# Second mixer of a two-model kernel: halves of queries and keys exchanged by transfers instead of a product, and two pairs of score banks for the differential attention

## The chip, the core and the metric

The kernel runs on one core of a Trainium2 chip. A core has TensorE for matrix products (in the profile PE, its weight loads PEld), VectorE (DVE), ScalarE (ACT), GpSimd (POOL) and SyncE (SP, which issues most transfers). They run side by side and meet at semaphores. TensorE writes to PSUM, which has eight banks of 128 partitions by 512 fp32 numbers. The metric is device time in microseconds; less is better.

## The reference, cut to what matters

The program computes a first transformer block and then a second model of two layers, for one sequence of 512 tokens of width 1024. The first layer of the second model is the "even mixer": a state-space scan (Mamba 2) and a differential attention side by side. The change touches the attention's queries and keys, and how its scores are scheduled.

```python
def rope(x, pos):
    d = x.shape[-1]                      # 64
    half = d // 2
    ang = pos.astype(F32)[:, :, None] * inv_freq
    x1, x2 = xf[..., :half], xf[..., half:]
    return jnp.concatenate([x1 * cos - x2 * sin, x2 * cos + x1 * sin], axis=-1)

def diff_attention_group(q, k, v, pos, layer, lambdas, subln):
    q = rope(q.reshape(bsz, s, 2 * hh, d), pos).reshape(bsz, s, hh, 2, d)   # hh = 8 heads, d = 64
    k = rope(k.reshape(bsz, s, 2 * hh, d), pos).reshape(bsz, s, hh, 2, d)
    ...
        p1 = masked_softmax(einsum('bqhd,bkhd->bhqk', q1b, k1) * scale, mask)
        p2 = masked_softmax(einsum('bqhd,bkhd->bhqk', q2b, k2) * scale, mask)
        return einsum('bhqk,bkhe->bqhe', p1 - lam * p2, vf)
    o = rms_norm_2(o, subln) * (1.0 - lam_init)
```

Each head has two queries and two keys of 64 numbers. The rope multiplies a vector by a cosine and adds its two halves of 32, exchanged and one of them negated, times a sine.

## The kernel before

Activations lie with features on partitions and the 512 tokens along the free axis. Every dense product is done in split precision: a weight panel is loaded by SP to `w_raw`, ScalarE casts it to `w_hi` (line 1296), GpSimd subtracts to `w_lo` (line 588), and TensorE does three products for each tile of 128 features (lines 617 to 619, or 638 to 640 where tokens are on the partitions of the result). Five slots of weights rotate. The order of panels is written out in `ORDER`, and each engine's program is written by hand in the order in which it runs; an engine that waits at a semaphore holds everything behind it in its program.

In the second mixer two loops of 32 steps each run one after the other, and dense products are filled in between ("units", one generator step each, about 0.70 us of TensorE).

The scan (lines 948 to 960 on TensorE): in step s TensorE does half of the step's units, then `segments(s+1)` (lines 935 and 937, banks 4 and 5), then the rest of the units, waits for `s_m`, and does the value products (line 958). ScalarE takes the exponential of the segments (line 1580), VectorE multiplies them (line 2295). `SSM_FILL` says how many units a step takes. `segments(s+1)` waits until ScalarE has read the banks, by `s_e`. The units compute the queries and keys of head groups 0 and 1 (`dqk0`, `dqk1`, four tiles each) and their values (`dv0`, `dv1`). On ScalarE and VectorE, `DONE_SSM` says after which step a tile is dealt with: ScalarE copies it from PSUM to `QD` (line 1566) and casts the next panels; VectorE does the rope (lines 2264, 2266, 2267).

The attention (`attend_diff`): the units are the same for groups 2 and 3, and then the tiles `out2a`, 168 entries by `DIFF_FILL`. For step c (a head and a block of 128 queries, with 128 to 512 keys) TensorE does `scores(c)` (lines 978 and 966, banks 4 and 5), VectorE the two maxima (lines 2310 and 2311), ScalarE the two exponentials (line 1600), VectorE the probabilities (lines 2344 to 2347), TensorE their transposes (line 1022), and ScalarE copies those (line 1631). In step c TensorE does half of the units, `scores(c+1)`, which waits for both exponentials of step c, the other half, and then waits for the probabilities of step c. Once in each head come the value sums (line 991), a sum of squares and a spread root.

The halves are exchanged by `rotate(i)`: TensorE multiplies a tile of queries or keys by the fp32 matrix `rot64` into bank 2 (line 908), 16 times in all, each counted as one entry of the filling. `rope(i)` on VectorE multiplies that by the sine. Bank 3 takes the first half of the values of each group (`dv0` to `dv3`), so no pair of banks is free for a second pair of scores.

`MLA`, in the second layer, uses the same semaphores `s_rot` and `s_rotf` for its own rotation, counted on from 16.

## Time and profile before

| | us |
|---|---|
| median of 3 runs | 2554.46 (2553.76 to 2554.94) |
| the profiled execution | 2556.53 |
| its span | 2554.7 |
| scan, 32 steps (1168.5 to 1291.2) | 122.7 |
| attention, 32 steps (1291.2 to 1491.5) | 200.3 |
| mean granted TensorE clock | 0.985 |

TensorE is busy 97% of the span, VectorE 51%, GpSimd 42%, ScalarE 34%. The page divides the span in 40 slices; the two loops lie in slices 19 to 24. In a row of the timeline the first number is the start in us from the beginning of the span, the second the length, then engine, line, operation and operands, and in brackets the idle time before it and what ended that. In the windows view each engine has its busy time and in parentheses the instructions; behind them stand the granted clock as a share of 2.4 GHz, the share of the DMA engines and GB/s. An fp32 product with a 128x512 operand is recorded as two matmuls.

### The profile page before, as it was taken

Reading aid. Unit: us, or ns where it says so; the run is one execution under the profiler, and the core shown is the slowest. Engines: PE = TensorE matmul, PEld = TensorE weight load, DVE = VectorE, ACT = ScalarE, POOL = GpSimd, SP = SyncE. Lnnn points to the kernel's source line nnn. Section 1 sums busy time; section 2 is a strip of 40 time slices with the busy share of each in tenths; the row PEclk is TensorE's granted clock in tenths of the full one; section 3 lists DMA queues with packets and bytes.
Section 4 is the critical chain, followed back from the end, with each engine's and each line's share of the span. In section 5 each row is a group of like instructions: output and inputs, shape, how many; then the busy total and the mean of one; then the engine's idle time right before and its main releaser. Section 6 shows DMA issues by size and latency. Waiting matters only on the chain.

```text
span 2554.7 us, 30093 instructions
## 1 busy us (share of the span) xinstructions
PE 2469.6 (97%) x11694; PEld 1976.1 (77%) x11694; DVE 1296.2 (51%) x1928; ACT 868.2 (34%) x1360; POOL 1061.4 (42%) x830
## 2 busy tenths in 40 slices
PE   8999999999999999999989999999999889999998
PEld 6877667888888888876767778888888756788886
DVE  6336687533633321585757655586126865533301
ACT  4453246222322222244444433322224353322221
POOL 4323244654544445353222245455453222544442
PEclk9999999999999999999999999999998999999999
DMA  4212122322332333221111123332331112222232
GB/s 147 69 56 77 62 72 87 99 93 89 111 96 94 99 94 96 95 79 58 50 50 50 50 74 106 99 99 90 97 98 51 31 34 64 98 99 92 95 98 78
DMA packets 62573, 209.44 MB, mean 82 GB/s; under 512 B 6880, under 2 KB 9184, under 8 KB 62304
## 3 DMA queue, kind: packets, MB, share of 16 engines
q1 hardware_dynamic: 61424, 204.11, 25.0%
q10 hardware_dynamic: 1008, 3.41, 0.4%
q8 instruction: 93, 1.52, 0.2%
q14 instruction: 48, 0.39, 0.0%
HBM read 205.39 MB, written 2.10 MB: 81 GB/s over the span
## 4 chain that ended last, share of the span: by engine, by line
PE 86%; DVE 10%; ACT 2%; issue 2%; DMA 0%; DVEq 0%; ACTq 0%; SPq 0%
PE ps L617 24%; PE ps L619 24%; PE ps L618 24%; DVE T L2163 1%; PE ps L638 1%; PE ps L639 1%; PE ps L640 1%; PE ps L958 1%; PE ps L734 1%; ACT A L1600 1%; PE ps L725 1%; PE ps L991 1%; PE ps L978 1%; PE ps L812 1%; DVE small L2310 1%
## 5 line engine op out<-in xcount | busy, mean ns | idle before, releaser
L588 POOL TENSOR_TENSOR w_lo<-w_raw,w_hi 128x512 fp32r<-128x512 f32 (+4 forms) x822 | 1051.6, 1303 | 1454.9 <-ACT w_hi L1296 1454.7
L617 PE MATMUL ps<-H,w_hi 128*128 128x512 f32 x1880 | 756.5, 402 | 22.6 <-DVEq L1858 11.7
L619 PE MATMUL ps<-H,w_lo 128*128 128x512 f32 x1880 | 738.0, 393 | 0.0
L618 PE MATMUL ps<-H,w_hi 128*128 128x512 f32 x1880 | 737.2, 392 | 0.0
L1296 ACT CAST w_hi<-w_raw 128x1024 fp32r<-128x1024 f32 (+4 forms) x411 | 402.9, 984 | 523.7 <-DMA w_raw<-in_weights_dram 517.4
L617 PEld LDWEIGHTS ps<-H,w_hi 128*128 128x128 f32 x1880 | 356.1, 189 | 115.6 <-issue 24.4
L617 PE MATMUL ps<-split,w_hi 128*128 128x512 f32 x1034 | 411.5, 398 | 6.8 <-issue 3.3
L619 PEld LDWEIGHTS ps<-H,w_lo 128*128 128x128 f32 x1880 | 355.7, 189 | 75.8
L618 PEld LDWEIGHTS ps<-H,w_hi 128*128 128x128 f32 x1880 | 356.3, 190 | 73.2 <-issue 2.6
L619 PE MATMUL ps<-split,w_lo 128*128 128x512 f32 x1034 | 403.7, 390 | 0.0
L618 PE MATMUL ps<-split,w_hi 128*128 128x512 f32 x1034 | 403.5, 390 | 0.0
L1881 DVE TENSOR_TENSOR T<-ps,R 128x512 f32<-128x512 f32 x164 | 113.4, 691 | 411.7 <-PE ps L619 407.2
L617 PEld LDWEIGHTS ps<-split,w_hi 128*128 128x128 f32 x1034 | 194.5, 188 | 55.5 <-issue 11.7
L619 PEld LDWEIGHTS ps<-split,w_lo 128*128 128x128 f32 x1034 | 194.5, 188 | 40.9
L618 PEld LDWEIGHTS ps<-split,w_hi 128*128 128x128 f32 x1034 | 194.7, 188 | 40.3 <-issue 1.7
L1888 DVE TENSOR_TENSOR X<-X,ps 128x512 f32<-128x512 f32 x48 | 33.0, 687 | 332.4 <-PE ps L619 330.8
L1310 ACT ACTIVATE SQ<-X 128x512 f32<-128x512 f32 x49 | 31.0, 632 | 211.3 <-DVEq L1890 198.6
L1483 ACT ACTIVATE T<-T 128x512 f32<-128x512 f32 x66 | 41.7, 632 | 170.9 <-DVEq L2130 170.9
L2133 DVE TENSOR_TENSOR T<-T 128x512 f32<-128x512 f32 x66 | 78.3, 1186 | 9.7
L638 PE MATMUL ps<-w_hi,H 128*128 128x256 f32 x256 | 78.3, 306 | 0.0
L639 PE MATMUL ps<-w_lo,H 128*128 128x256 f32 x256 | 72.4, 283 | 0.0
L640 PE MATMUL ps<-w_hi,H 128*128 128x256 f32 x256 | 72.2, 282 | 0.0
(405 smaller groups left out, 2401.1 us busy)
## 6 DMA issues: line engine op xcount, KB each, us to landing
w_raw<-in_weights_dram SPq DMA_DIRECT2D x323, 512.0 KB, 3.5
w_raw<-in_weights_dram SPq DMA_DIRECT2D x48, 448.0 KB, 3.2
w_raw<-in_weights_dram SPq DMA_DIRECT2D x22, 256.0 KB, 2.6
X<-in_xt_dram SPq DMA_DIRECT2D x4, 512.0 KB, 7.8
out_dram<-A SPq DMA_DIRECT2D x8, 256.0 KB, 2.1
w_raw<-in_weights_dram SPq DMA_DIRECT2D x12, 128.0 KB, 2.0
w_raw<-in_weights_dram SPq DMA_DIRECT2D x6, 192.0 KB, 2.3
A<-in_w_gates_dram ACTq DMA_DIRECT2D x1, 1024.0 KB, 4.9
```

The source lines that it names most:

```text
L588: sub = nc.gpsimd.tensor_tensor(w_lo[:, p % NS, c], w_raw[:, p % NS, c], w_hi[:, p % NS, c].bitcast(F32), ALU.subtract)
L617: mm_(ps[:, bank, :], r(wh), xh, start=(k == 0), stop=False)
L618: mm_(ps[:, bank, :], r(wh), xl, start=False, stop=False)
L619: mm = mm_(ps[:, bank, :], r(wl), xh, start=False, stop=(k == kt - 1))
L638: mm_(o, xh, r(wh), start=(k == 0), stop=False)
L639: mm_(o, xh, r(wl), start=False, stop=False)
L640: mm = mm_(o, xl, r(wh), start=False, stop=(k == kt - 1))
L1296: nc.scalar.copy(w_hi[:, p % NS, 0:PSIZE[p]], w_raw[:, p % NS, 0:PSIZE[p]]).then_inc(w_hi_ready[p % NS], 1)
L1483: A_(T[:, j % 2, :], T[:, j % 2, :], ACT.Silu).then_inc(s_silu, 1)
L1881: link(v.tensor_tensor(dst, ps[:, bank, :], R, ALU.mult))
L1888: link(v.tensor_tensor(X[:, t, :], X[:, t, :], ps[:, bank, :], ALU.add))
L2133: link(v.tensor_tensor(T[:, 2 + q, :], T[:, 2 + q, :], T[:, q, :], ALU.mult))
```

## The change

The constant `rot64` and `rotate` are gone. After ScalarE has copied a tile to `QD`, it issues four transfers of 32 partitions each (`swap_halves`), which write the tile with its halves exchanged to `ROPE_T`, from SBUF to SBUF. Before them it waits for `s_swapf`: the rope of the tile before, which reads the one buffer `ROPE_T`. VectorE's `rope(i)` waits for the transfers and multiplies `ROPE_T` by the sine in place. The sign is now in the sine (`sign64`, folded in where the sine is scaled). `DONE_SSM` and `DONE_DIFF` put the rope of tile n-1 in the same step as the copy of tile n.

Without rotations the filling has 96 entries in the scan (3 a step) and 160 in the attention. The values of groups 2 and 3 go to banks 0 and 1 and are copied in two halves (`dv_half`). Banks 2 and 3 become a second pair for scores: in step c TensorE does `scores(c+2)`, which waits for the exponentials of step c, and VectorE does the maxima of c+2. `MLA` counts its semaphores from 0.

```diff
@@ -44,8 +44,8 @@
     "dt": (1, (8,), 128, (4,)), "xbc": (12, (8,), 128, (0, 1, 2, 3)), "z": (8, (8,), 128, (0, 1, 2, 3)),
     "dqk0": (4, (8,), 128, (0, 1)), "dv0": (1, (4, 4), 256, (3, 0)),
     "dqk1": (4, (8,), 128, (1, 0)), "dv1": (1, (4, 4), 256, (3, 1)),
-    "dqk2": (4, (8,), 128, (0, 1)), "dv2": (1, (4, 4), 256, (3, 0)),
-    "dqk3": (4, (8,), 128, (1, 0)), "dv3": (1, (4, 4), 256, (3, 1)),
+    "dqk2": (4, (8,), 128, (0, 1)), "dv2": (1, (4, 4), 256, (0, 1)),
+    "dqk3": (4, (8,), 128, (0, 1)), "dv3": (1, (4, 4), 256, (0, 1)),
...
@@ -441,6 +438,10 @@
         S5H = [[h_tile(10 + 2 * i), h_tile(11 + 2 * i)] for i in range(2)]
         S5T = [h_tile(14), h_tile(15)]
         S5_BANKS = (4, 6)
+
+        def diff_banks(c):
+
+            return ((4, 5), (2, 3))[c % 2]
...
 
         def dqkv_items(p):
             name = f"dqk{p}"
-            return [((name, 0), 8), ((name, 1), 8), (("rot", 4 * p), 1), ((name, 2), 8), (("rot", 4 * p + 1), 1),
-                    ((name, 3), 8), (("rot", 4 * p + 2), 1), (("part", p), 12), (("rot", 4 * p + 3), 1),
+            return [((name, 0), 8), ((name, 1), 8), (("rot", 4 * p), 0), ((name, 2), 8), (("rot", 4 * p + 1), 0),
+                    ((name, 3), 8), (("rot", 4 * p + 2), 0), (("dv_half", p), 8), (("part", p), 4), (("rot", 4 * p + 3), 0),
                     ((f"dv{p}", 0), 4)]
 
-        SSM_FILL = (3, 3, 3, 4)
+        SSM_FILL = (3, 3, 3, 3)
         DONE_SSM = steps_done(dqkv_items(0) + dqkv_items(1), SSM_FILL, 32)
-        DIFF_FILL = (12,) + (4, 5, 5, 5) * 7 + (5, 5, 5)
+        DIFF_FILL = (12,) + (4, 5, 5, 4) * 7 + (5, 5, 4)
...
                             mm = mm_(o, xl, r(wh), start=False, stop=(k == kt - 1))
-                            if tile[0] == "v_b" and q == 1 and k == kt - 1:
+                            if tile[0] in ("v_b", "dv2", "dv3") and q == 1 and k == kt - 1:
...
-            def rotate(i):
-                p, n = divmod(i, 4)
-                pe.wait_ge(s_qc, i + 1)
-                if i >= 1:
-                    pe.wait_ge(s_rotf, i)
-                mm_(ps[:, 2, :], con("rot64"), QD[p][:, n, :], start=True, stop=True).then_inc(s_rot, 1)
-
             def fill_dqkv(p):
                 for n in range(4):
                     yield from units((f"dqk{p}", n), HX)
@@ -914,14 +909,7 @@
                         norm_cols("gate", 7)
                     if p == 2 and n == 1:
                         norm_spread("gate", 7, RTG)
-                    if n:
-                        rotate(4 * p + n - 1)
-                        yield
-                for u, _ in enumerate(token_units((f"dv{p}", 0), HX)):
-                    yield
-                    if u == 11:
-                        rotate(4 * p + 3)
-                        yield
+                yield from token_units((f"dv{p}", 0), HX)
...
-                if c >= 1:
-                    pe.wait_ge(s_ex, 2 * c)
+                banks = diff_banks(c)
+                if c == 1:
+                    pe.wait_ge(bank_free[3], uses_through(3, "dv1"))
+                if c >= 2:
+                    pe.wait_ge(s_ex, 2 * c - 2)
                 for a in range(2):
                     rows = slice(64 * a, 64 * a + 64)
-                    mm_(ps[:, 4 + a, 0:w], QD[p][rows, hh, P * i:P * i + P], QD[p][rows, 2 + hh, 0:w],
+                    mm_(ps[:, banks[a], 0:w], QD[p][rows, hh, P * i:P * i + P], QD[p][rows, 2 + hh, 0:w],
                         start=True, stop=False)
                 for a in range(2):
-                    chunk_mask(4 + a, a, w)
...
             def attend_diff(fill):
                 scores(0)
+                scores(1)
                 for c in range(32):
                     head, i = c // 4, c % 4
                     n = DIFF_FILL[c % len(DIFF_FILL)]
                     run(fill, n // 2)
-                    if c + 1 < 32:
-                        scores(c + 1)
+                    if c + 2 < 32:
+                        scores(c + 2)
                     run(fill, n - n // 2)
...
 
             def rotate_mla(i):
                 if i:
-                    pe.wait_ge(s_rotf, 16 + i)
+                    if i:
+                        pe.wait_ge(s_rotf, i)
...
+            def swap_halves(p, t):
+                if p or t:
+                    act.wait_ge(s_swapf, 4 * p + t)
+                else:
+                    act.wait_ge(s_dtn, 1)
+                    act.wait_ge(s_csr, 1)
+                for b in range(4):
+                    other = 32 * (b ^ 1)
+                    act.dma_start(ROPE_T[32 * b:32 * b + 32, :], QD[p][other:other + 32, t, :]).then_inc(s_swap, 16)
+
             def copy_dqkv(tile):
                 name, t = tile
                 if name in ("rot", "part", "spread"):
+                    return
+                if name == "dv_half":
+                    if t >= 2:
+                        hi_to(last_panel(f"dv{t}") + 2)
+                        act.wait_ge(s_vhalf, t + 1)
+                        copy_rows((f"dv{t}", 0), lambda q: VD[t][:, q, :], None, rows=range(2))
                     return
                 if name == "cols":
                     root("gate", 7)
@@ -1566,8 +1575,9 @@
                     link(nc.scalar.copy(QD[p][:, t, :], ps[:, bank, :]))
                     act.sem_inc(bank_free[bank], 1)
                     act.sem_inc(s_qc, 1)
+                    swap_halves(p, t)
                 else:
-                    copy_rows(tile, lambda q: VD[p][:, q, :], s_vd)
+                    copy_rows(tile, lambda q: VD[p][:, q, :], s_vd, rows=range(2 if p >= 2 else 0, ST))
...
-                    link(A_(EX[:, 2 * (c % 2) + a, 0:w], ps[:, 4 + a, 0:w], ACT.Exp,
+                    link(A_(EX[:, 2 * (c % 2) + a, 0:w], ps[:, diff_banks(c)[a], 0:w], ACT.Exp,
...
-                    link(v.tensor_tensor(SIN, SIN, R, ALU.mult))
+                    link(v.scalar_tensor_tensor(SIN, SIN, con("sign64"), R, ALU.mult, ALU.mult))
...
             def rope(i):
                 p, n = divmod(i, 4)
                 x = QD[p][:, n, :]
-                dve.wait_ge(s_rot, i + 1)
-                link(v.tensor_tensor(ROPE_T, ps[:, 2, :], SIN, ALU.mult))
-                dve.sem_inc(s_rotf, 1)
+                dve.wait_ge(s_swap, 64 * i + 64)
+                link(v.tensor_tensor(ROPE_T, ROPE_T, SIN, ALU.mult))
                 link(v.tensor_tensor(x, x, COS, ALU.mult))
                 link(v.tensor_tensor(x, x, ROPE_T, ALU.add))
+                dve.sem_inc(s_swapf, 1)
                 dve.sem_inc(s_roped, 1)
...
-                    link(v.tensor_reduce(small[:, b + a:b + a + 1], ps[:, 4 + a, 0:w], AX.X, ALU.max))
+                    link(v.tensor_reduce(small[:, b + a:b + a + 1], ps[:, diff_banks(c)[a], 0:w], AX.X, ALU.max))
...
             maxima(0)
+            maxima(1)
             for c in range(32):
                 head, i = c // 4, c % 4
                 w = P * i + P
@@ -2346,8 +2357,8 @@
                 link(v.tensor_scalar(e1, e1, small[:, b + 2:b + 3], None, ALU.mult))
                 v.scalar_tensor_tensor(e1, e2, small[:, b + 3:b + 4], e1, ALU.mult, ALU.add).then_inc(s_pn, 1)
                 beside_diff(c - 1)
-                if c < 31:
-                    maxima(c + 1)
+                if c < 30:
+                    maxima(c + 2)
```

## Rows read from the trace of the kernel before

**Rows 1.** Page of the profile, part 1: busy time and its share.

```profile
PE 2469.6 (97%) x11694; PEld 1976.1 (77%) x11694; DVE 1296.2 (51%) x1928; ACT 868.2 (34%) x1360; POOL 1061.4 (42%) x830
```

**Rows 2.** Windows view: length of stretch, busy time by engine, granted clock, DMA share.

```profile
1168.50:1291.20 122.70, 120.69 (x658) 83.61 (x658) 79.29 (x123) 54.56 (x99) 33.08 (x24) 1.00 0.16 49
1291.17:1491.50 200.33, 188.17 (x1025) 142.31 (x1025) 129.58 (x288) 94.15 (x228) 52.11 (x38) 0.97 0.17 52
```

**Rows 3.** Timeline of PE around two rotations: start, length, line, operands.

```profile
1198.69 1.02 PE L908 MATMUL ps<-A,C_ 128*128 128x512 f32 x2
1199.64 0.44 PE L958 MATMUL ps<-T,A 128*64 128x128 f32 x4
...
1376.44 1.02 PE L908 MATMUL ps<-A,C_ 128*128 128x512 f32 x2
1377.30 0.27 PE L1022 MATMUL ps<-C_,A 128*128 128x128 f32 x1
```

**Rows 4.** Waits view, 1290 to 1492 us: total us, times, longest.

```profile
ACT A L1600 <- DVE small L2311: 78.2, 30, 4.7
...
PE ps L978 <- ACTq L1602: 10.0, 9, 3.0
...
PE ps L991 <- DVEq L1851: 1.8, 1, 1.8
...
PE ps L978 <- DVEq L2279: 1.5, 1, 1.5
```

**Rows 5.** Timeline of PE: the segment products of scan steps 11 and 13.

```profile
1208.20 0.23 PE L935 MATMUL ps<-CS,CR 80*128 80x128 f32 x1
...
1215.78 0.34 PE L935 MATMUL ps<-CS,CR 80*128 80x384 f32 x1
```

**Rows 6.** Timeline of ACT in scan steps 11 and 12.

```profile
1210.31 1.05 ACT L1296 CAST w_hi<-w_raw 128x1024 fp32r<-128x1024 f32 x1 [0.18 <-ACT A L1566]
1212.96 1.26 ACT L1580 ACTIVATE T<-ps,small 128x512 f32<-128x512 f32 x2 [1.60 <-PE ps L937]
```

**Rows 7.** Timeline of DVE in scan step 11: the split, then the rope.

```profile
1209.50 0.48 DVE L1856 TENSOR_SCALAR split<-A,V_ 128x512 fp32r<-128x512 f32 x1
...
1211.75 0.69 DVE L2264 TENSOR_TENSOR A<-ps,A 128x512 f32<-128x512 f32 x1
...
1213.34 1.67 DVE L2267 TENSOR_TENSOR A<-A 128x512 f32<-128x512 f32 x1
```

**Rows 8.** Source view of two lines: the issues of transfers, ns min/median/max.

```profile
L1428 ACTq DMA_DIRECT2D A<-in_w_gates_dram x1: 339/339/339, 206.2 to 206.2; - x1
...
L562 SPq DMA_DIRECT2D X<-in_xt_dram x4: 423/530/536, 1.2 to 3.3; - x4
```

**Rows 9.** Timeline of PE: the wait before the second pair of scores.

```profile
1299.05 0.70 PE L978 MATMUL ps<-A 64*128 64x256 f32 x4 [3.03 <-ACTq L1602]
```

**Rows 10.** Timeline of ACT: exponentials of attention steps 2 and 3.

```profile
1313.65 0.58 ACT L1600 ACTIVATE A<-ps,small 128x384 f32<-128x384 f32 x1 [0.44 <-DVE small L2311]
...
1319.98 0.69 ACT L1600 ACTIVATE A<-ps,small 128x512 f32<-128x512 f32 x1 [2.67 <-DVE small L2311]
```

**Rows 11.** Timeline of DVE: the maxima of attention step 3.

```profile
1317.39 1.42 DVE L2310 TENSOR_REDUCE small<-ps 128x1 f32<-128x512 f32 x2
```

**Rows 12.** Windows view: two stretches at a lower clock, one without.

```profile
1300.70:1307.50 6.80, 6.80 (x21) 5.67 (x21) 1.52 (x6) 1.13 (x4) 0.00 (x0) 0.50 0.24 77
1399.70:1403.20 3.50, 3.50 (x10) 2.29 (x9) 1.97 (x8) 1.13 (x4) 0.00 (x0) 0.51 0.43 124
257.29:270.00 12.71, 12.64 (x53) 9.59 (x54) 11.40 (x17) 3.58 (x8) 2.99 (x2) 1.00 0.12 43
```

**Rows 13.** Timeline of PE: a wait in the first block.

```profile
257.29 0.50 PE L617 MATMUL ps<-H,w_hi 128*128 128x512 f32 x1 [2.85 <-DVEq L1882]
```

**Rows 14.** Source view of two rope operations: ns min/median/max.

```profile
L2264 DVE TENSOR_TENSOR A<-ps,A x16: 676/683/691, 1192.6 to 1422.6; 128x512 f32<-128x512 f32 x16
...
L2267 DVE TENSOR_TENSOR A<-A x16: 691/694/1704, 1194.2 to 1424.1; 128x512 f32<-128x512 f32 x16
```

More of the change, by code:

```diff
@@ L141 @@
 CONSTS = [
-    ("ident", 128), ("ones", 128), ("after", 128), ("upto", 128), ("rot64", 128), ("rot32", 128),
-    ("pool_inv", 64), ("eps", 1), ("freq64", 1), ("freq32", 1),
+    ("ident", 128), ("ones", 128), ("after", 128), ("upto", 128), ("rot32", 128),
+    ("pool_inv", 64), ("eps", 1), ("sign64", 1), ("freq64", 1), ("freq32", 1),
 ]
@@ L181, in constants @@
     c["chunk_rows"] = ((i[:, None] % 64 == 63) & (i[None, :] < 64)) * 1.0
-    rot = np.zeros((P, P))
-    for m in range(P):
-        rot[m + 32 if m % 64 < 32 else m - 32, m] = -1.0 if m % 64 < 32 else 1.0
-    c["rot64"] = rot
+    c["sign64"] = np.where(i % 64 < 32, -1.0, 1.0)[:, None]
     rot = np.zeros((P, P))
@@ L500, in build @@
         s_ang, s_sin = sem("angles_ready"), sem("sines_ready")
+        s_swap, s_swapf = sem("halves_swapped"), sem("halves_read")
         s_qc, s_vd, s_rot, s_rotf, s_roped = (sem("qk_copied"), sem("v_copied"), sem("rotated"), sem("rotated_read"),
@@ L973, in scores @@
                     pe.wait_ge(s_roped, 4 * p + 4)
-                if c >= 1:
-                    pe.wait_ge(s_ex, 2 * c)
+                banks = diff_banks(c)
[3 more added lines that the diff above has]
+                    pe.wait_ge(s_ex, 2 * c - 2)
                 for a in range(2):
                     rows = slice(64 * a, 64 * a + 64)
-                    mm_(ps[:, 4 + a, 0:w], QD[p][rows, hh, P * i:P * i + P], QD[p][rows, 2 + hh, 0:w],
+                    mm_(ps[:, banks[a], 0:w], QD[p][rows, hh, P * i:P * i + P], QD[p][rows, 2 + hh, 0:w],
                         start=True, stop=False)
                 for a in range(2):
-                    chunk_mask(4 + a, a, w)
+                    chunk_mask(banks[a], a, w)
             def value_sums(head):
@@ L1162, in regroup @@
                 else:
-                    pe.wait_ge(s_rotf, 16 + 3)
+                    pe.wait_ge(s_rotf, 3)
                 for i in range(TAPS):
@@ L2513, in rope_mla @@
                 tmp = S5T[0]
-                dve.wait_ge(s_rot, 16 + i + 1)
+                dve.wait_ge(s_rot, i + 1)
                 link(v.tensor_tensor(tmp, ps[:, 3, :], SINM, ALU.mult))
```

## Prediction

> **What bounds the kernel now.** I read the page first: TensorE is busy 97% of the span [rows 1], so a change gains what it takes off TensorE's program or out of its waits. The windows view of the two loops shows where waits are: in the scan TensorE is busy 120.7 of 122.7 us, in the attention 188.2 of 200.3 us with a mean clock of 0.97 [rows 2]. The waits view of the attention names them: 10.0 us in 9 waits before the scores (L978) for ScalarE's exponentials, the longest 3.0; 1.8 us before the last value sums (L991); 1.5 us for the gate before the first scores [rows 4]. ScalarE in its turn waits 78.2 us for the maxima [rows 4]: the loop scores, maxima, exponentials, probabilities has only one step of lead. In the scan no engine makes TensorE wait within the loop; ScalarE (54.6 us busy) and VectorE (79.3) have room there [rows 2], but room on average says nothing of an engine that is held for some us at one place.
>
> **Rotations.** A rotation takes TensorE from its start to the next start: 0.95 us in the scan (1198.69 to 1199.64), 0.86 in the attention (1376.44 to 1377.30) [rows 3]. Eight fall away in each loop. In the scan the last one lies behind the last segments, where the end is set by VectorE (gate, rope) and not by TensorE (the wait of 1.5 [rows 4]); TensorE would only come earlier to that wait. So 7 x 0.95 = 6.6 us there, and 8 x 0.86 = 6.9 us in the attention. The number of units before each wait stays nearly the same.
>
> **What is put on ScalarE's program.** A tile's copy is now followed by a wait for the rope of the tile before (`s_swapf`), four issues of transfers and then the cast; the next exponentials are queued behind all that. A single issue on ScalarE took 0.34 us, four of SP in a row 0.53 each (median) [rows 8]; nearest to this are those of ScalarE, so 4 x 0.34 with gaps = 1.5 us, at most 2.1. The transfers themselves, of 64 KB each, have at least one step until the rope reads them; I cost their landing at nothing, since the DMA engines are busy a sixth of the time [rows 2]. If they took over some 5 us, VectorE would wait.
>
> The wait is the dear part. In the scan the copy of tile n and the rope of tile n-1 fall in the same step, for n = 1, 2, 3 in steps 6, 8, 11 and again in 22, 24, 27 (8, 16, 24, 32 entries at 3 a step). Take step 11. TensorE starts its segments at 1208.20 and those of step 13 at 1215.78 [rows 5]; without the rotation in between that is 7.58 - 0.95 = 6.6 us. The segments of 13 need the exponentials of 12. VectorE's split starts at 1209.50, the rope behind it at 1211.75, its third operation at 1213.34 [rows 7]; at 0.69 us (median [rows 14]) it ends at 1214.0, 5.8 us after the segments. Then ScalarE: 0.15 for the semaphore, 1.5 for the issues, 0.18 + 1.05 for the cast, 0.63 for the first exponential (half of 1.26) [rows 6], together 9.4. TensorE waits 9.4 - 6.6 = 2.8 us, and 0.2 more for the second bank: 3.0. In steps 6 and 8 there is no split (2.25 us less [rows 7]), but longer multiplications or a square lie on the way; in the same manner I come to 1.3 and 1.4 us. Sum: 2 x (3.0 + 1.4 + 1.3) = 11.4 us. From both sides: 6.0 if only steps 11 and 27 count, 16.0 with 0.53 us for an issue (0.76 more at six places). A TensorE that is always busy never makes up such a wait.
>
> VectorE's first rope operation reads SBUF twice now, where it read PSUM. The row with PSUM never took over 0.69 us, the one with two SBUF operands up to 1.70 [rows 14], when GpSimd was subtracting. The Trainium skill, SBUF — State Buffer, section "SBUF: two separate sides", says that a VectorE operation with two SBUF inputs and a GpSimd operation that reads SBUF lock each other out of a shared port pair; by that the three waits of a group would grow by up to 1 us each. I take none of it, since GpSimd's work follows the cast, and the cast now comes behind the rope.
>
> **Opening of the attention.** The long wait of 3.0 us [rows 9] is ended by VectorE's chain (gate, split, maxima of step 0), which stays. In it TensorE now also does `scores(1)`, some 0.7 us [rows 9]. Gain 0.7.
>
> **The attention loop.** The wait of `scores(c+2)` stands at the same place as that of `scores(c+1)` did and is for the same exponentials, those of c. But their scores are done a step earlier, so the loop has two steps for what had one. That takes out the other 10.0 - 3.0 = 7.0 us and the 1.8 before the last value sums [rows 4]. What is late next is ScalarE's new work, at the head of the loop. In step 1 ScalarE copies the first tile, issues, casts and takes the gate's root with two table loads; the exponentials of step 2 stood at 1313.65 after 0.44 of waiting [rows 10], so they move to 1313.65 - 0.44 + 1.5 = 1314.7, and the spread of the root holds TensorE about 1.2 us. From the exponentials of step 2 to those of step 3 it took 6.3 us [rows 10]. This had the maxima of step 3, 2.6 us from 1317.39 [rows 11] to the exponential, which are now done before; in their place come the rope (2.3), the issues (1.5) and a cast (1.2): 8.7 us. So they start at 1323.4 and end 1.7 us later, at 1325.1. TensorE, with the same units, is at the scores of 5 at about 1320.7: a wait of 4.5 us. Followed on in the same way, later copies find room (steps 4, 6, 13, 15), and the one in step 16, right behind another, costs 1.0. New waits: 1.2 + 4.5 + 1.0 = 6.7 us.
>
> **The clock.** After the wait of 3.0 us the clock was at 1.2 GHz from 1300.7 to 1307.5, and after one of 1.9 from 1399.7 to 1403.2 [rows 12]; at half speed these cost 3.4 and 1.7 us. The second wait goes: 1.7 us gained. After the wait of 2.85 us in the first block [rows 13] it stayed at 2.4 GHz [rows 12], so a wait of about 3 us may or may not bring it down. There are three new ones (3.0, 3.0, 4.5), and the one of 3.0 is shortened. I put one more fall than now, at 2.5 us (the mean of the two), and 0 to four as bounds.
>
> **Sum.** Scan: + 6.6 - 11.4 = -4.8. Opening + 0.7. Attention: 6.9 + 7.0 + 1.8 + 1.7 - 6.7 = + 10.7. Clock - 2.5. Together 4.1 us less. The profiled execution took 2556.5 us (a span of 2554.7 and 1.8 around it), 2.1 more than the median. 2556.5 - 4.1 = 2552.4, and for the median 2550. The change pays in the attention and takes back half of it in the scan.
>
> **Rivals.** (B) ScalarE is held less: only steps 11 and 27 make TensorE wait, and the clock stays up. For it speaks that the waits in steps 6 and 8 are small differences of long sums. 6.6 - 6.0 + 0.7 + 10.7 = 12.0 less: 2542.
>
> (C) Slower: ScalarE's blocked exponentials in the scan. Price: issues at 0.53 us make the six waits 16.0, and the clock falls after the long ones, four times 2.5. 6.6 - 16.0 + 0.7 + 10.7 - 10.0 = -8.0: 2562. It decides from the point where scan waits and clock together pass 18.0 us; my sum has 13.9. Against it: a wait of 2.85 us without a fall. The Trainium skill speaks for it: TensorE: Matmul & The Clock Gate, section "HAM oscillation — how this bites in real kernels", tells of a kernel whose TensorE waits between short bursts, and each burst starts at half rate.
>
> (D) The wait for the rope holds nothing, because VectorE is early: 6.6 + 0.7 + 6.9 + 7.0 + 1.8 + 1.7 = 24.7 less, 2530. Against it stand the times of step 11.
>
> (E) The second pair doesn't do what it says: ScalarE's exponentials stay the last to arrive through the loop, as the wait is for the same ones. Then 10.5 us (7.0 + 1.8 + 1.7) stay in place of the 6.7: 0.3 less, 2554. Against it speaks that ScalarE spends 78.2 us on the maxima [rows 4], which now come a step ahead.
>
> **How the numbers follow.** The forecast, 2550 with its own range 2545 to 2555, has 0.43; B 0.24, C 0.15, D 0.06, E 0.08, and 0.04 for a time near no change from elsewhere. A measurement of this kernel tells about 0.2%, 5.1 us, from no change, so the forecast lies by that border: of its 0.43 I give 0.18 to faster and 0.25 to the same. Faster: 0.18 + 0.24 + 0.06 = 0.48. The same: 0.25 + 0.08 + 0.04 = 0.37. Slower: 0.15. The range takes in B and nearly C: 2540 to 2561; outside are D and part of C.
>
> **What would show it.** L908 is gone from the profile. In the scan, the segments (L935) wait for ScalarE's exponentials (L1580 before) about 3 us in steps 12 and 28 and some 1.4 in 7, 9, 23, 25; if they wait under 1 us everywhere, B or D holds. ScalarE shows four issues behind each copy: their length decides between B and C. In the attention one wait of 4 to 5 us before the scores of step 5, and nearly none behind it; ScalarE's wait for maxima far below 78 us. If the waits at L978 keep 7 us outside the opening, E holds. The clock is to be below 1.0 at two or three places in the two loops; at five or more, C. The prediction is wrong if ScalarE isn't what TensorE waits for in the scan, or if the transfers land so late that VectorE waits for them.

## The result, and the profile after

| | before | after |
|---|---|---|
| median, us (5 runs each) | 2553.76 (2546.22 to 2554.94) | 2572.64 (2566.82 to 2578.68) |
| ratio, 95% interval | | 1.0084 [1.0065, 1.0102] |
| the profiled execution | 2556.53 | 2566.82 |
| scan (first segments to first scores) | 122.7 | 145.7 |
| attention (first scores to the end of the value sums) | 202.4 | 197.9 |

The change made the kernel slower by 0.84%, 18.9 us. The forecast was 2550, the range up to 2561: wrong in sign, and outside the range. The two loops took 325.1 us before and 343.6 after, 18.5 more.

The profiled pair differs by only 10.3 us. The main reason is a stretch of 24 us in the second layer in the execution of before, which that of after had not (windows view of before):

```profile
1928.00:1952.00 24.00, 24.00 (x95) 21.44 (x95) 9.81 (x15) 7.55 (x15) 5.02 (x4) 0.57 0.07 22
```

The work there is the same in both kernels but for how `MLA` counts its semaphores, and one of the experiments below had such a stretch too. So I lay nothing of it to the change, and read differences between kernels from the two loops first and from the medians second.

The windows view of after, the counterpart of [rows 2] (length, busy PE, PEld, DVE, ACT, POOL, clock, DMA share, GB/s):

```profile
1170.60:1316.29 145.69, 126.25 (x641) 87.69 (x641) 85.26 (x123) 55.26 (x100) 33.45 (x25) 0.91 0.20 58
1316.29:1512.08 195.79, 181.68 (x1008) 140.12 (x1009) 130.79 (x288) 91.10 (x226) 49.45 (x38) 0.97 0.20 60
```

TensorE is busy 126.3 us in the scan with fewer instructions than before (641 to 658), and the clock stands at 0.91 instead of 1.00. Beside that it now stands still for 19.4 us. The waits view of after says why (total us, times, longest), first the scan, then the attention, against [rows 4]:

```profile
PE ps L923 <- ACT T L1590: 15.0, 7, 4.2
PE ps L946 <- DVE T L2305: 1.0, 2, 0.5
ACT w_hi L1289 <- issue: 39.9, 8, 7.1
```

```profile
PE ps L969 <- ACTq L1612: 11.0, 5, 5.1
PE ps L969 <- DVEq L2289: 3.2, 1, 3.2
PE ps L676 <- DVEq L1880: 2.1, 1, 2.1
PE ps L982 <- DVEq L1861: 0.9, 1, 0.9
ACT A L1610 <- DVE small L2321: 3.4, 1, 3.4
```

L923 are the segments (L935 before), L946 the value products, L969 the scores (L978 before), L676 the spread of the root, L982 the value sums. In the scan TensorE waits 15.0 us for ScalarE's exponentials, where it had waited 0.3; ScalarE in turn stands 39.9 us, in eight places, ahead of the cast (L1289) behind the new wait and the issues. In the attention the second pair does its part: ScalarE waits 3.4 us for maxima where it waited 78.2. Yet TensorE still waits 11.0 us for the exponentials, in five places.

The source view of the issue (ns min/median/max), and its landing:

```profile
L1552 ACTq DMA_DIRECT2D A<-A x64: 514/612/1400, 1182.5 to 1429.9; - x64
...
DMA to landing us min/median/max: 1.9/2.0/3.9
```

An issue took 0.61 us, not the 0.34 of [rows 8]; the transfers land in 2.0 us, and no engine waits for them.

Steps 11 and 12 of the scan in the timelines of after, the counterpart of [rows 5 to 7]. TensorE, VectorE, ScalarE:

```profile
1216.22 0.23 PE L923 MATMUL ps<-CS,CR 80*128 80x128 f32 x1
...
1226.18 0.69 PE L923 MATMUL ps<-CS,CR 80*128 80x384 f32 x1 [3.05 <-ACT T L1590]
```

```profile
1217.06 0.55 DVE L2305 TENSOR_TENSOR T<-T,A 128x128 f32<-128x128 f32 x2 [1.05 <-ACT T L1590]
...
1219.78 0.69 DVE L2274 TENSOR_TENSOR A<-A 128x512 f32<-128x512 f32 x1
...
1221.23 0.69 DVE L2276 TENSOR_TENSOR A<-A 128x512 f32<-128x512 f32 x1
```

```profile
1222.01 2.44 ACTq L1552 DMA_DIRECT2D A<-A  x4
1224.49 1.04 ACT L1289 CAST w_hi<-w_raw 128x1024 fp32r<-128x1024 f32 x1 [6.34 <-issue]
1225.45 1.26 ACT L1590 ACTIVATE T<-ps,small 128x512 f32<-128x512 f32 x2
```

This is the chain that the prediction worked out: the rope ends 5.7 us after the segments, then issues, cast, first exponential, and TensorE has waited 3.05 us. At most of these waits, but not at all of them, the granted clock goes to 0.5, and the busy time of the scan swells. The windows view, behind the waits of 1.4 and 1.2 us in the scan, around that of 4.2 us, and behind that of 2.1 us (L676) in the attention:

```profile
1201.50:1204.50 3.00, 3.00 (x10) 1.79 (x9) 2.82 (x5) 1.04 (x2) 0.34 (x1) 0.51 0.11 11
...
1270.00:1276.00 6.00, 5.90 (x29) 4.24 (x31) 5.59 (x8) 2.16 (x5) 1.92 (x2) 1.00 0.29 87
1279.00:1286.00 7.00, 4.27 (x12) 3.02 (x14) 4.14 (x4) 2.88 (x5) 2.82 (x2) 0.54 0.14 33
...
1336.00:1342.00 6.00, 5.99 (x35) 4.81 (x36) 4.74 (x10) 3.17 (x7) 0.65 (x1) 1.00 0.08 30
```

There are five stretches at 1.2 GHz in the scan and three in the attention, where before had two in all. To sum them I cut the loops into windows of 2 us and add (1 - clock) x 2: 13.6 us in the scan and 6.8 in the attention, against 0 and 5.1. I call this sum the clock loss below. It counts a window at half clock also while TensorE stands, so it lies a little above what the busy time grew by.

### The profile page after: what moved, and what is told of

It reads as the page before. It is cut to its first block, busy times and chain, and to the rows that moved or that the text cites. A ratio compares the mean times of both kernels' runs of the same rounds, so it can differ in the third digit from the quotient of the medians.

```text
span 2565.0 us, 30079 instructions
## 1 busy us (share of the span) xinstructions
PE 2460.3 (96%) x11662; PEld 1972.2 (77%) x11662; DVE 1306.7 (51%) x1928; ACT 865.8 (34%) x1360; POOL 1059.1 (41%) x830
## 4 chain that ended last, share of the span: by engine, by line
PE 84%; DVE 10%; issue 2%; ACT 2%; ACTq 1%; DMA 0%; DVEq 0%; SPq 0%
PE ps L619 24%; PE ps L621 24%; PE ps L620 24%; DVE T L2173 1%; ACTq L1552 1%; PE ps L640 1%; PE ps L641 1%; PE ps L642 1%; PE ps L969 1%; DVE T L2305 1%; PE ps L736 1%; PE ps L727 1%; PE ps L814 1%; PE ps L982 1%; PE ps L761 1%
## 5 line engine op out<-in xcount | busy, mean ns | idle before, releaser
L619 PE MATMUL ps<-H,w_hi 128*128 128x512 f32 x1880 | 758.1, 403 | 22.4 <-DVEq L1868 12.5
L1289 ACT CAST w_hi<-w_raw 128x1024 fp32r<-128x1024 f32 (+4 forms) x411 | 402.9, 984 | 592.4 <-DMA w_raw<-in_weights_dram 516.6
L621 PEld LDWEIGHTS ps<-split,w_lo 128*128 128x128 f32 x1034 | 194.1, 188 | 40.9
L620 PEld LDWEIGHTS ps<-split,w_hi 128*128 128x128 f32 x1034 | 194.3, 188 | 39.9 <-issue 1.7
L640 PE MATMUL ps<-w_hi,H 128*128 128x256 f32 x256 | 78.5, 307 | 0.0
L2305 DVE TENSOR_TENSOR T<-T,A 128x512 f32<-128x512 f32 (+3 forms) x64 | 44.9, 741 | 58.9 <-ACT T L1590 57.8
```

What stands on the lines that cost most here:

```text
L619: mm_(ps[:, bank, :], r(wh), xh, start=(k == 0), stop=False)
L620: mm_(ps[:, bank, :], r(wh), xl, start=False, stop=False)
L621: mm = mm_(ps[:, bank, :], r(wl), xh, start=False, stop=(k == kt - 1))
L640: mm_(o, xh, r(wh), start=(k == 0), stop=False)
L1289: nc.scalar.copy(w_hi[:, p % NS, 0:PSIZE[p]], w_raw[:, p % NS, 0:PSIZE[p]]).then_inc(w_hi_ready[p % NS], 1)
L2305: v.tensor_tensor(t, t, GM[:, pair // 4, TRI[i]:TRI[i + 1]], ALU.mult).then_inc(s_m, 1)
```

## The experiments

Each kernel is the changed one with the alteration shown (two in the kernels that combine them). They were timed in three rounds, each on another chip and beside the kernel before, whose median was 2552.8, 2553.6 and 2552.2 us. A ratio is to the before of its own round; differences in microseconds are between medians, or between the loops of one profiled execution of each. The theory: ScalarE's program is held behind each copy (wait for the rope, then four issues), which makes TensorE wait, and each such wait tends to bring the clock down. The rivals: the issues alone; the wait alone; a gain of the second pair of banks that is not there; transfers that are late or load the DMA engines.

| kernel | median us | ratio to before, 95% | scan | attention | clock loss of the loops | rest of the profiled execution (its clock loss) |
|---|---|---|---|---|---|---|
| before | 2553.8 | | 122.7 | 202.4 | 5.1 | 2231.4 (30.7) |
| after | 2572.6 | 1.0084 [1.0065, 1.0102] | 145.7 | 197.9 | 20.5 | 2223.2 (22.4) |
| no exchange at all | 2522.8 | 0.9893 [0.9868, 0.9919] | 118.2 | 181.3 | 1.7 | 2220.6 (18.9) |
| two buffers | 2530.4 | 0.9921 [0.9898, 0.9945] | 121.5 | 185.0 | 1.7 | 2222.4 (18.5) |
| SyncE issues | 2527.6 | 0.9907 [0.9883, 0.9932] | 118.0 | 181.4 | 1.7 | 2229.3 (29.4) |
| one issue in place of four | 2535.6 | 0.9941 [0.9917, 0.9964] | 128.5 | 186.8 | 8.6 | 2220.2 (18.6) |
| rotations kept in the scan | 2544.5 | 0.9976 [0.9963, 0.9989] | 122.7 | 196.6 | 5.1 | 2223.5 (22.3) |
| one pair of banks | 2575.4 | 1.0096 [1.0066, 1.0125] | 145.0 | 208.7 | 23.9 | 2220.8 (18.8) |
| SyncE issues, ScalarE waits | 2534.1 | 0.9936 [0.9915, 0.9958] | 123.5 | 183.2 | 3.4 | 2236.3 (37.3) |
| SyncE issues, one pair | 2542.4 | 0.9969 [0.9956, 0.9982] | 118.1 | 199.1 | 8.5 | 2224.5 (23.4) |
| cast ahead of the wait | 2560.0 | 1.0049 [1.0027, 1.0071] | 142.7 | 194.1 | 20.4 | 2220.1 (17.2) |

The last column is what the profiled execution took outside the two loops. Less its clock loss it is 2199 to 2204 us in all eleven kernels, and 2200.8 in before as in after: the change moved nothing there but the clock, which differs between executions by up to 20 us. The two longest stretches at a low clock, of 24 us in before and 26 in "SyncE issues, ScalarE waits" (from 1914, mean clock 0.54), lie at the same place, some 435 us behind the attention. Before's own times fall into two groups: in the last round, six of 14 at 2543.3 to 2548.5 us with a mean clock of 0.989 to 0.991, eight at 2552.1 to 2556.5 with 0.985 to 0.987. So a difference of medians holds some microseconds that no edit explains.

### No exchange at all

```diff
                     act.sem_inc(s_qc, 1)
-                    swap_halves(p, t)
...
-                link(v.tensor_tensor(ROPE_T, ROPE_T, SIN, ALU.mult))
+                link(v.tensor_tensor(ROPE_T, x, SIN, ALU.mult))
```

> The kernel after without the exchange: no transfer is issued, and the rope multiplies the tile itself by the sine (this part of the result is left out). Theory 1 (ScalarE is held behind each copy, by the wait for the rope and four issues of 0.61 us each, and the clock falls in the waits of TensorE that follow): the scan falls from 145.7 to about 116 us (122.7 of the kernel before less seven rotations of 0.95) with a clock of 1.00, the waits before the segments are under 1 us together, and the kernel is some 20 us faster than before. Rival (without rotations TensorE's clock falls anyhow, or the second pair of banks costs something by itself): the scan keeps a clock below 0.95, or the attention stays near 196 us though ScalarE is free.

2522.8 us: 30 less than before in its round, where some 20 were expected; the scan, 118.2, and the waits are near what the theory said. TensorE's waits for exponentials in the scan are gone (waits view of this kernel), and the clock is 1.00:

```profile
PE ps L923 <- ACT T L1589: 0.3, 1, 0.3
```

So everything that the change lost, and more, hangs on the exchange; whether on what it puts on ScalarE or on the transfers themselves, this kernel can't say. Without it, the rotations and the second pair are worth 25.6 us in the two loops (325.1 - 299.5); the medians of its round show 4.4 us more, less than what the clock varies by outside the loops. The wait of 3.2 us for the gate, before the first scores, stays in this kernel and in all that take the rotations out of the scan.

### Two buffers: the issues stay, the wait goes

```diff
-                if p or t:
-                    act.wait_ge(s_swapf, 4 * p + t)
+                if 4 * p + t > 1:
+                    act.wait_ge(s_swapf, 4 * p + t - 1)
...
-                    act.dma_start(ROPE_T[32 * b:32 * b + 32, :], QD[p][other:other + 32, t, :]).then_inc(s_swap, 16)
+                    act.dma_start(rope_t(4 * p + t)[32 * b:32 * b + 32, :], QD[p][other:other + 32, t, :]
+                                  ).then_inc(s_swap2[t % 2], 16)
```

> Two buffers for the exchanged tile, so that ScalarE waits for the rope of two tiles before, which is done; the four issues on ScalarE stay. If the wait for the rope is what pushes the exponentials past their time: copy, issues (2.45), cast (1.2) and the first exponential end some 6.3 us after the segments of step 11 where TensorE comes at 6.6, so the waits in the scan fall from 15 us to under 2, the scan to 116 to 119 us with a clock of 1.00, and the kernel is 15 to 19 us faster than before. If the issues alone are too long: the waits stay above 6 us in the scan, and it takes over 125 us.

2530.4 us, 22 less than before in its round, where 15 to 19 were expected; the scan, 121.5, is above the 116 to 119. The same 64 issues of the same length stay on ScalarE (source view), what ScalarE stands ahead of the cast falls from 39.9 to 21.8 us, little more than the issues, and TensorE waits no longer for exponentials in the scan; 3.0 us in small waits of the value products remain:

```profile
L1555 ACTq DMA_DIRECT2D A<-A x48: 514/612/622, 1179.7 to 1384.1; - x48
...
PE ps L949 <- DVE T L2310: 3.0, 6, 0.6
PE ps L926 <- ACT T L1594: 0.3, 1, 0.3
```

(The row has 48; the other 16 write to the second buffer of the attention and stand in a row of their own.) Issues alone are cheap beside what both cost: against the next kernel they are 7.1 us in the loops (306.5 to 299.4) and 2.8 in the medians (2530.4 to 2527.6), whose intervals overlap. The rival "issues alone" falls.

### SyncE issues: neither on ScalarE

The same four transfers, issued by SyncE between its loads of weights, five panels behind the tile's last.

```diff
+            swaps = {last_panel(f"dqk{g}", t) + 5: (g, t) for g in range(4) for t in range(4)}
             for p in range(2, PANELS):
                 panel(p)
+                if p in swaps:
+                    g, t = swaps[p]
+                    sp.wait_ge(s_qc, 4 * g + t + 1)
+                    if g or t:
+                        sp.wait_ge(s_swapf, 4 * g + t)
...
+                    for b in range(4):
+                        other = 32 * (b ^ 1)
+                        sp.dma_start(ROPE_T[32 * b:32 * b + 32, :], QD[g][other:other + 32, t, :]).then_inc(s_swap, 16)
...
                     act.sem_inc(s_qc, 1)
-                    swap_halves(p, t)
```

> The same transfers, issued by SyncE behind the panel that the finished tile makes room for; ScalarE neither waits nor issues. Theory 1: as without the exchange, scan about 116 us, 17 to 20 us faster than before. Rival (the transfers themselves are the cost: they hold up the weights, or land so late that VectorE waits): the weights come late, TensorE waits for GpSimd or VectorE at the rope, and the scan stays over 122 us.

2527.6 us, 25 less than before in its round (17 to 20 were expected) and 45 less than after, with the whole computation in it and one buffer. The loops are 25.7 us shorter than before's and 44.2 shorter than after's. Windows and waits views of this kernel:

```profile
1173.60:1291.60 118.00, 113.97 (x640) 81.12 (x640) 85.27 (x123) 55.61 (x100) 33.91 (x24) 1.00 0.24 72
...
PE ps L981 <- DVEq L2300: 3.2, 1, 3.2
...
PE ps L935 <- ACT T L1601: 0.3, 1, 0.3
```

Its 640 instructions of the scan take TensorE 114.0 us at full clock; in after 641 of the same take 126.3. So of the 27.7 us between these two scans 12.3 are the clock, and nearly all the rest are waits. The transfers are the same, and the DMA engines are busier than in after (0.24 to 0.20): the rival "transfers" falls.

### SyncE issues, and ScalarE waits all the same

Beside SyncE's issues as above (its `swaps`), `swap_halves` keeps its waits and loses its transfers:

```diff
                     act.wait_ge(s_dtn, 1)
                     act.wait_ge(s_csr, 1)
-                for b in range(4):
-                    other = 32 * (b ^ 1)
-                    act.dma_start(ROPE_T[32 * b:32 * b + 32, :], QD[p][other:other + 32, t, :]).then_inc(s_swap, 16)
```

> SyncE issues the four transfers, as in the kernel where only that was changed (2527.6 us), but ScalarE keeps its wait for the rope of the tile before, at its place behind the copy. So the wait is priced without the issues. In the changed kernel TensorE waited 1.4, 1.8, 3.1, 1.2, 4.2 and 3.0 us at the six places of the scan, with 2.5 us of issues in each. If wait and issues only add up on one chain (my theory), 2.5 us less leave 0.6, 1.7 and 0.5, together 3 us, with one fall of the clock at most: 2530 to 2535 us, scan about 121. If the wait alone is what costs (rival), the scan keeps at least 8 us of waits and three or more stretches at half clock, and the time is above 2545.

2534.1 us, within the 2530 to 2535 of the theory; the scan is 123.5 where it had about 121. Waits view of the scan:

```profile
PE ps L935 <- ACT T L1599: 2.1, 4, 0.7
PE ps L958 <- DVE T L2314: 1.9, 4, 0.5
ACT w_hi L1301 <- DVEq L2286: 18.4, 6, 3.9
```

ScalarE still stands 18.4 us for the rope, but TensorE notices 2.1. Against the kernel in which SyncE issues and ScalarE has neither, the loops show 7.3 us for the wait alone (306.7 to 299.4), 7.1 for the issues alone and 44.2 for both; the medians 6.5, 2.8 and 45. The two small prices lie within the noise of the medians (intervals [0.9915, 0.9958], [0.9898, 0.9945] and [0.9883, 0.9932]), the large one far outside. Neither is "the" cause: each uses up slack that the other needs, and the chain of the two passes the time that TensorE has between two segments.

### One issue in place of four

Here the halves are not exchanged, one transfer of 128 partitions copies the tile; the wait for the rope stays.

```diff
-                for b in range(4):
-                    other = 32 * (b ^ 1)
-                    act.dma_start(ROPE_T[32 * b:32 * b + 32, :], QD[p][other:other + 32, t, :]).then_inc(s_swap, 16)
+                act.dma_start(ROPE_T, QD[p][:, t, :]).then_inc(s_swap, 16)
```

> One transfer of 128 partitions in place of four of 32 (it copies the tile and doesn't exchange its halves: this part of the result is left out); the wait for the rope stays. Issue time falls from 2.45 to 0.6 us. Theory 1, with the wait and the issues adding up on ScalarE: the waits of about 3.05 and 1.8 us fall to about 1.2 and 0, the scan to 117 to 122 us, and the clock doesn't fall there; 10 to 17 us faster than before. If the wait for the rope is what counts and not the issues: over 8 us of waits stay in the scan.

2535.6 us, 17 less than before in its round, the upper end of what was expected (10 to 17). But the scan, 128.5, is above the 117 to 122, and the clock did fall in it (3.4 us), which the theory had excluded. Timeline of ScalarE and waits view of the scan:

```profile
1200.75 0.47 ACTq L1550 DMA_DIRECT2D A<-A  x1
...
PE ps L923 <- ACT T L1588: 5.0, 5, 1.7
```

Between no issue, 0.47 us and 2.44 us behind the same wait, TensorE's waits for the exponentials of the scan go 2.1, 5.0, 15.0. From one issue to four the chain is 2.0 us longer; at six places that is 12, and the waits grew by 10. That fits a sum on one chain in size, though 5.0 us of waits were left where 1.2 at each of two places were expected. The clock loss of both loops grew by 11.9 beside it.

### Cast ahead of the wait

```diff
+                    hi_to(last_panel(name, t) + 5)
                     swap_halves(p, t)
```

> The changed kernel with one change of order on ScalarE: the casts of the next panels come ahead of the wait for the rope and the issues, not behind them. If what delays the exponentials is the moment at which the rope ends (theory), the cast of 1.1 us is hidden in that wait, and the six waits of TensorE in the scan go from 15 us to 8 to 10, with fewer falls of the clock: scan 132 to 138 instead of 145.7, in all 2555 to 2563 us. If the rope then meets GpSimd's subtraction and gets slower by as much, or if the cast was not on the chain, the scan stays within 3 us of 145.7 and the time near 2570.

The time, 2560.0 us, is where the theory had it, but not for its reason: the scan is 142.7, not 132 to 138, with 15.3 us of waits. The timelines of VectorE and GpSimd in the step that answers to the one above show what the hidden cast cost:

```profile
1212.46 1.55 DVE L2275 TENSOR_TENSOR A<-A 128x512 f32<-128x512 f32 x1
1214.04 1.65 DVE L2276 TENSOR_TENSOR A<-A 128x512 f32<-128x512 f32 x1
```

```profile
1212.15 3.00 POOL L590 TENSOR_TENSOR w_lo<-w_raw,w_hi 128x512 fp32r<-128x512 f32 x2 [8.00 <-ACT w_hi L1289]
```

The cast released GpSimd's subtraction, and while that ran (to 1215.15) two rope operations took 1.55 and 1.65 us in place of 0.69: 1.8 us given back for a cast of 1.05 hidden. The Trainium skill, SBUF — State Buffer, section "SBUF: two separate sides", states a lock on a shared port pair between a VectorE operation with two SBUF inputs and a GpSimd operation that reads SBUF; the trace agrees, with 1.55 and 1.65 us in place of 0.69. So the rival of this run holds for the scan. Why the attention gained 3.8 us I have not traced. Of the 12.7 us between the medians the two loops show 6.8; in the profiled pair another 5.2 are the clock outside them (22.4 to 17.2).

### One pair of score banks, with and without ScalarE's burden

```diff
-            return ((4, 5), (2, 3))[c % 2]
+            return (4, 5)
...
-                if c >= 2:
-                    pe.wait_ge(s_ex, 2 * c - 2)
+                if c >= 1:
+                    pe.wait_ge(s_ex, 2 * c)
...
-                    if c + 2 < 32:
-                        scores(c + 2)
+                    if c + 1 < 32:
+                        scores(c + 1)
```

(and the maxima one step ahead). First with ScalarE issuing, as in after:

> The exchange by transfers as after, but one pair of score banks and one step of lead, as before. The scan as after, 145 us. If the second pair does what it says: in the attention the maxima come behind the rope again, TensorE waits more than the 11 us before the scores of the kernel after and more than the 10 us of the kernel before, the attention takes 205 to 215 us, and the kernel is 28 to 40 us slower than before. If the second pair brings nothing: the attention takes about 196 us, as after.

Then with SyncE issuing:

> SyncE issues the transfers, and there is one pair of score banks, with the scores one step ahead, as before the change. So the second pair is priced while ScalarE is free. With one pair the kernel before waited 10.0 us for the exponentials, 3.0 of them in the opening, and 1.8 before value sums, and lost 5.1 us of clock; the attention then takes 200.3 - 6.9 (rotations) = 193.4 us against 181.4 with two pairs: 12 us more, 2540 us. Rival: with ScalarE free the second pair is worth as little as the medians of the changed kernel showed (2.7 us): 2530.

The waits for exponentials in the attention, of the first and of the second kernel:

```profile
PE ps L967 <- ACTq L1609: 15.1, 9, 4.5
```

```profile
PE ps L979 <- ACTq L1620: 11.8, 8, 5.0
```

With ScalarE free the second pair is worth 2542.4 - 2527.6 = 14.8 us, 17.7 in the attention (199.1 to 181.4): more than the 12 expected, since part of it is clock (8.5 to 1.7). The intervals of these two ratios don't overlap. With ScalarE held the attention is 10.8 longer with one pair (208.7 to 197.9), within the 205 to 215 expected, but the medians differ by only 2.7: the kernel is 22 us slower than before in its round, where 28 to 40 were expected. The intervals of those two ratios overlap, so in the medians the size stays unsettled there. That the pair does what it says is settled.

### Rotations kept in the scan

Groups 0 and 1 are rotated by TensorE in the scan as before; the attention is as in after.

```diff
-            return [((name, 0), 8), ((name, 1), 8), (("rot", 4 * p), 0), ((name, 2), 8), (("rot", 4 * p + 1), 0),
+            if p < 2:
+                return [((name, 0), 8), ((name, 1), 8), (("rot", 4 * p), 1), ((name, 2), 8), (("rot", 4 * p + 1), 1),
...
+                if p < 2:
+                    dve.wait_ge(s_rot, i + 1)
+                    link(v.tensor_tensor(ROPE_T, ps[:, 2, :], SIN, ALU.mult))
```

> Rotations by TensorE in the scan as before, transfers and two pairs of score banks in the attention as after. Theory 1: the scan takes 122.7 us as before with a clock of 1.00; the attention as after, about 196 us, or some 3 us less if the clock doesn't fall at its head; together 4 to 8 us faster than before. Rival (the loss of the change comes from the attention or from what both share): the scan is long even with rotations, or the kernel is not faster than before.

2544.5 us, 9.1 less than before in its round, where 4 to 8 were expected. The scan takes 122.7 us with the clock at 1.00, as before: the whole loss of 23 us there came with the transfers. In the attention the waits stay, much as in after:

```profile
PE ps L991 <- ACTq L1632: 11.4, 6, 3.7
```

5.8 us of the gain are in the attention (202.4 to 196.6), although ScalarE still carries the burden there; with SyncE issuing that loop gains 21.0 (202.4 to 181.4). The rest of the gain lies outside the loops.

## Why the prediction was wrong, point by point

**Bound and rotations: right.** TensorE bounds the loops, and 6.6 us for the scan's rotations holds: 120.69 - 6.6 = 114.1 us of busy time, and the kernel with SyncE issues has 113.97. That TensorE would only come earlier to the gate holds too (1.5 us became 3.2), but this longer wait brings the clock down behind it, 1.7 us that I had not counted.

**Issues: mis-sized.** 1.5 us for four, at most 2.1; measured 2.44. I took the issue of a load from DRAM for one of 32 partitions from SBUF to SBUF; the row I set aside, 0.53, was the nearer.

**Scan waits: right in place, too small at one.** All six waits are where the prediction has them. In steps 7, 9, 12, 23, 25 and 28 TensorE waited 1.39, 1.80, 3.05, 1.22, 4.16 and 3.04 us, against 1.3, 1.4, 3.0, 1.3, 1.4 and 3.0. Together 14.7 (15.0 with a small one at the start) against 11.4; 2.8 of the 3.3 are step 25. That the other five agree so closely is in part luck. With the issues at their measured 2.44 my working would have come to 11.4 + 6 x 0.94 = 17.0. At step 12 the chain was only 0.5 longer than I had it (9.9 to 9.3; I wrote 9.4), as the rope ended 0.1 earlier and the gaps between ScalarE's instructions were shorter, and TensorE itself came 6.9 us after its segments and not 6.6. The timeline of TensorE, five of the six (the row of step 12 stands above):

```profile
1200.03 0.50 PE L923 MATMUL ps<-CS,CR 80*128 80x512 f32 x1 [1.39 <-ACT T L1590]
1210.82 0.39 PE L923 MATMUL ps<-CS,CR 80*128 80x256 f32 x1 [1.80 <-ACT T L1590]
...
1270.10 0.50 PE L923 MATMUL ps<-CS,CR 80*128 80x512 f32 x1 [1.22 <-ACT T L1590]
1281.73 0.58 PE L923 MATMUL ps<-CS,CR 80*128 80x256 f32 x1 [4.16 <-ACT T L1590]
1297.46 0.69 PE L923 MATMUL ps<-CS,CR 80*128 80x384 f32 x1 [3.04 <-ACT T L1590]
```

Ahead of step 25, VectorE and GpSimd:

```profile
1270.08 1.99 DVE L2305 TENSOR_TENSOR T<-T,A 128x128 f32<-128x128 f32 x2 [4.43 <-ACT T L1590]
...
1273.40 0.69 DVE L1872 TENSOR_TENSOR ACC<-ACC,SQ 128x512 f32<-128x512 f32 x1
```

```profile
1269.34 2.58 POOL L590 TENSOR_TENSOR w_lo<-w_raw,w_hi 128x512 fp32r<-128x512 f32 x2 [9.91 <-ACT w_hi L1289]
```

VectorE got the exponentials of step 23 late, since ScalarE had just been held, and multiplied them (1.99 us) while GpSimd subtracted behind the late cast; the same two multiplications take 0.55 in step 11 (1217.06), so that is 1.4 us. The split and a sum of squares (0.69), which I had not at this place, followed, then the second pair of multiplications, and the rope came behind them all and ended at 1277.6. I had set each place on the undisturbed trace of before, as if it were the first; a held queue hands its delay on. I had also said that the lock between VectorE and GpSimd would cost nothing, as the cast comes behind the rope. The source view of two of the rope's operations shows how far that held:

```profile
L2274 DVE TENSOR_TENSOR A<-A x16: 683/687/1542, 1193.2 to 1443.2; 128x512 f32<-128x512 f32 x16
...
L2276 DVE TENSOR_TENSOR A<-A x16: 691/692/693, 1194.7 to 1444.6; 128x512 f32<-128x512 f32 x16
```

The rope was spared nearly everywhere (L2267 had gone up to 1.70 before [rows 14]); the multiplication behind the cast was not.

**The clock: the step that failed.** I put one more fall than now at 2.5 us, beside 1.7 gained. Net that is 0.8 us. Measured: eight falls against two, 15.4 us of clock loss more; that is the larger part of the error of 22.6 us, and enough by itself to turn the sign. I had read from [rows 12, 13] that a wait of 3 us may or may not bring the clock down, and then priced nine new waits as if it nearly never would. At five of the six long waits of the scan it fell, the shortest 1.39 us. The Trainium skill, TensorE: Matmul & The Clock Gate, section "HAM oscillation — how this bites in real kernels", tells of a kernel that begins its bursts at half rate, each behind a wait; here that came at these five waits and not at that of 1.22 us. I had cited it for rival C alone.

The row that I leaned on was one draw of several. The wait of 2.85 us in the first block [rows 13] stands in all eleven profiled executions, 2.82 to 2.85 us long and with the same work before it. In before, "two buffers", "SyncE issues, ScalarE waits" and "cast ahead of the wait" the clock stayed at 1.00 behind it; in the other seven it fell to 0.5 there. The timeline and windows views of after:

```profile
259.08 0.80 PE L619 MATMUL ps<-H,w_hi 128*128 128x512 f32 x1 [2.82 <-DVEq L1892]
...
259.00:263.00 4.00, 3.92 (x12) 3.29 (x13) 3.65 (x8) 0.41 (x2) 0.00 (x0) 0.58 0.02 4
```

So a wait of this length has no fixed price. It is a chance of a fall, and nine new waits need such a chance each.

**Attention: right in kind, too small.** The waits of before for the maxima went, as forecast, and the wait of 3.0 us in the opening too, which I had only shortened by 0.7. The new ones: 2.1 us at the spread (forecast 1.2), 5.1 at the scores of step 5 (4.5), and 0.7, 1.6, 1.0 and 2.7 for later exponentials, where I had a single one of 1.0. TensorE and ScalarE in after:

```profile
1348.19 1.22 PE L969 MATMUL ps<-A 64*128 64x256 f32 x4 [5.10 <-ACTq L1612]
```

```profile
1342.98 2.44 ACTq L1552 DMA_DIRECT2D A<-A  x4
1345.46 1.04 ACT L1289 CAST w_hi<-w_raw 128x1024 fp32r<-128x1024 f32 x1 [6.03 <-issue]
```

**The sum by its terms.** By my terms, without the 2.5 for the clock, the scan comes to 122.7 - 6.6 + 11.4 = 127.5. It took 145.7, 18.2 more: clock 12.2 (the busy time is 126.3 where 120.7 - 6.6 = 114.1 was due), waits for exponentials 3.3, the longer wait for the gate 1.7, value products 1.0. The clock loss of 13.6 is larger than 12.2, as the clock fell within some of the waits, which costs nothing; 1.1 of it lies in the wait of 4.16. The attention comes to 202.4 - 0.7 - 10.7 = 191.0 and took 197.9, 6.9 more: waits 14.0 in place of 9.0 (the 3.0 of the opening less 0.7, and 6.7), clock 3.4 more than I left it, and 1.5 the other way that I can't place. 18.2 + 6.9 - 2.5 = 22.6 us, and the median lies 22.6 above the forecast. That it agrees to the tenth is luck, with profiled executions that lie 2.8 above and 5.8 below their medians.

**Rivals.** C (0.15) had the mechanism, its place and its sign; its point was "scan waits and clock together pass 18.0 us", and they made 28.6. Its price, 2562, was too low for the same reason as the forecast: four falls of 2.5. D, the wait that holds nothing, shows what the freed ScalarE gives: 2530 forecast, 2527.6 with SyncE issuing. B falls, as TensorE waited over 1 us at all six places. E's sign, 7 us of waits before the scores outside the opening, was met with 11.0 us, but not for its reason: with SyncE issuing, the waits view shows none of TensorE for exponentials before the scores, so what remained was ScalarE's new work and not the loop.

## What to carry to other kernels

Look on whose in-order queue a wait for another engine stands, and work out the longest chain behind it against the time that the bounding engine has between two of its own waits: a wait and four issues that cost some 7 us each alone, in the loops, cost 44 together. Put them on a queue on which nobody waits, here SyncE's, or break the wait with a second buffer. And where a nearly full TensorE gets new waits like these, of 1.4 to 5.1 us, price a chance of a fall of the clock at each of them, and don't take one row without a fall for the rule; in the scan the clock cost nearly as much as the waits themselves (12.3 and 15.0 us).

## What the runs showed of the hardware that I had not expected

- An issue of a transfer of 32 partitions from SBUF to SBUF held ScalarE 0.61 us (median of 64; 0.51 to 1.40), one of 128 partitions 0.47; a load issued on ScalarE had taken 0.34. SyncE needs as long (2.4 us for four), but there nobody waits.
- The length of one wait doesn't tell whether the clock falls: it fell to 0.5 behind 1.39 and 1.80 us and stayed at 1.00 behind 2.13, in one execution; and behind the same wait of 2.82 to 2.85 us it fell in seven of eleven executions. What decides between them I haven't tested.
- Outside the two loops, where the eleven kernels do nearly the same work, the clock loss of a profiled execution was 17.2 to 37.3 us.
- At half clock the next wait shrinks, since TensorE comes later to it: between the segments issued in steps 7 and 9 (1200.03 and 1210.82), with the clock low, it worked 9.0 us and then waited 1.80; between those issued in steps 23 and 25, at full clock, 7.5 us and then 4.16.
